# Two 64-wide halves of TensorE at a time in the stick-breaking and retention stages of a two-block model

## The reference, cut to what matters

```python
def retention(q, k, v):                      # 4 heads of 128
    s = einsum('bhid,bhjd->bhij', qi, ki) * decay[None]
    intra = einsum('bhij,bhjd->bhid', s, vi)
    ...
def stick_breaking(q, k, v):                 # 8 heads of 64
    z = einsum('bhid,bhsd->bhis', qi, kh) * scale
    past = kpos[None, :] < qpos[:, None]
    log_keep = where(past, log_sigmoid(-z), 0.0)
    between = cumsum(log_keep, axis=3, reverse=True) - log_keep
    a = where(past, exp(log_sigmoid(z) + between), 0.0)
    return einsum('bhis,bhsd->bhid', a, vh)
def even_mixer(x, w_in, w_out):
    ret = silu(rg) * normalised(retention(rotary(rq), rotary(rk), rv))
    return concatenate([ret, stick_breaking(sq, sk, sv)], -1) @ w_out
```

## Time and profile before

| | us |
|---|---|
| median of 3 runs | 3577.01 (3575.97 to 3581.78) |
| the profiled execution, its own time | 3577.77 |
| its span from first to last record | 3575.7 |
| PE busy / DVE / ACT / GpSimd | 3069.0 / 2069.7 / 847.5 / 695.4 |
| retention matmuls, 2274.7 to 2306.2 | 31.5 |
| normalisation of retention, 2306.2 to 2318.7 | 12.5 |
| stick-breaking, 2318.7 to 2414.5 | 95.8 |

### The profile page before, as it was taken

One profiled execution on the slowest core, in us unless ns is written; L12 is line 12 of the kernel. 1 busy time (PEld: TensorE's weight loads), 2 busy tenths in 40 slices (PEclk: granted clock), 3 DMA queues, 4 the chain that ended last, 5 costly groups with the idle time before them and its releaser, 6 DMA issues. The chain is left out here.

```text
span 3575.7 us, 35397 instructions
## 1 busy us (share of the span) xinstructions
PE 3069.0 (86%) x12578; PEld 2058.9 (58%) x12578; DVE 2069.7 (58%) x3639; ACT 847.5 (24%) x2182; POOL 695.4 (19%) x670
## 2 busy tenths in 40 slices
PE   6999888987777777777777789989999999899998
PEld 4887667773223222222222257667888777678886
DVE  2323775567776764684444455246875374768743
ACT  2112433123222222222222221241211012422101
POOL 0001443004444444444333311000000000200000
PEclk9999999999999999999999999989999999999999
DMA  7888896669999999999999942101332232023322
GB/s 246 283 268 272 244 295 217 198 234 422 421 421 421 419 414 421 416 409 420 417 421 420 419 169 90 43 1 48 109 96 90 93 100 65 1 83 94 99 88 71
DMA packets 154292, 845.78 MB, mean 237 GB/s; under 512 B 15328, under 2 KB 15584, under 8 KB 87584
## 3 DMA queue, kind: packets, MB, share of 16 engines
q0 software_dynamic: 79040, 561.28, 38.4%
q1 hardware_dynamic: 75104, 282.57, 25.2%
HBM read 841.70 MB, written 136.31 MB: 274 GB/s over the span
## 5 line engine op out<-in xcount | busy, mean ns | idle before, releaser
L798 PE MATMUL PS<-AR,HC 128*128 128x512 f32 x1536 | 721.1, 614 | 258.6 <-ACT HC L1272 257.2
L199 PE MATMUL PS<-AR_r,RHI 128*128 128x512 f32 x1888 | 752.3, 398 | 40.1 <-DVE AR_r L1444 13.6
L201 PE MATMUL PS<-AR_r,RING_r 128*128 128x512 f32 x1888 | 738.2, 391 | 0.0
L798 PEld LDWEIGHTS PS<-AR,HC 128*128 128x128 f32 x1536 | 281.1, 192 | 697.8 <-ACT HC L1272 404.1
L1627 DVE SCALAR_TENSOR_TENSOR AR<-AR 128x1024 f32<-128x1024 f32 x384 | 470.2, 1225 | 363.3 <-DMA AR<-peer_uv,XC 359.9
L200 PE MATMUL PS<-AR_r,RHI 128*128 128x512 f32 x1504 | 586.0, 390 | 0.0
L476 POOL DMA_INDIRECT AR<-peer_uv,XC x384 | 398.6, 1038 | 739.3 <-PE PS L798 547.8
L1426 DVE CAST RHI<-RING 128x1024 fp32r<-128x1024 f32 x256 | 178.7, 698 | 479.6 <-DMA RING<-in_wstream 476.9
L199 PEld LDWEIGHTS PS<-AR_r,RHI 128*128 128x128 f32 x1888 | 356.6, 189 | 124.8 <-issue 39.5
L201 PEld LDWEIGHTS PS<-AR_r,RING_r 128*128 128x128 f32 x1888 | 356.4, 189 | 75.1
L1428 DVE TENSOR_TENSOR RING_r<-RING,RHI 128x1024 fp32r<-128x1024 f32 x256 | 315.8, 1234 | 8.8
(11 more groups left out here) (336 smaller groups left out, 3492.4 us busy)
## 6 DMA issues: line engine op xcount, KB each, us to landing
RING<-in_wstream SPq DMA_DIRECT2D x304, 512.0 KB, 3.7
peer_uv<-in_peer_u SPq DMA_DIRECT2D x56, 1024.0 KB, 12.9
peer_uv<-in_peer_v SPq DMA_DIRECT2D x56, 1024.0 KB, 13.8
peer_uv<-in_peer_v POOLq DMA_DIRECT2D x8, 1024.0 KB, 13.3
peer_uv<-in_peer_u POOLq DMA_DIRECT2D x8, 1024.0 KB, 12.5
AR<-peer_uv,XC POOLq DMA_INDIRECT x384, 13.6
XL<-in_xl SPq DMA_DIRECT2D x1, 2048.0 KB, 9.4
RHI_f<-peer_uv,XC POOLq DMA_INDIRECT x128
```

The source lines that it names most:

```text
L199: pe.matmul(out, sh, mh, start=start, stop=False)
L201: return pe.matmul(out, sl, mh, start=False, stop=stop)
L798: mm = pe.matmul(bank(2 * (tt % 2) + x), DIAG[:, n % NDIAG, :], ROWS_UV[n % NROW][:, D + 512 * x:D + 512 * x + 512], start=(j == 0), stop= ...
```

## The change

Four things change.

1. Retention works on two heads at a time: `rt_scores(t)` makes the four matmuls of heads 2 pair and 2 pair + 1 alternately on the two row halves, into banks (0, 1) or (2, 7); `rt_values(t)` follows one step later with both heads. `SDEC` has four buffers in place of three.
2. GpSimd copies `SBQ` and `SBK` with four DMAs, right behind barrier 10, into `XC` and `HC` with the two halves of the partitions exchanged (512 KB each). The first `sb_scores` waits for all four. The four diagonal blocks of a head are computed from the exchanged copy, on the other 64 rows than the six later blocks, and the two kinds alternate in the order.
3. `sb_values(p)` computes two heads at a time, alternating the two halves of the output partitions, once for two heads. It stands behind `sb_weights(h)` of h = 2, 4, 6 and at the end, and `SBA` has three buffers. `sb_exp(h)` then waits for a values step only from h = 3 on.
4. DVE copies 128 partitions once for two heads (`sb_out(p)`), 4 copies in place of 8.

```diff
--- before.py
+++ after.py
@@ -315,7 +315,10 @@
         RO = EW[:, 0:2048].rearrange("p (a b) -> p a b", a=4)
         RSQ = HLF[:, 0:2048].rearrange("p (a b) -> p a b", a=4)
         RST = HLF[:, 2048:4096].rearrange("p (a b) -> p a b", a=4)
-        SBL, SBP, SBA = [HLF[:, 0:SBW], EW[:, 0:SBW]], [HLF[:, SBW:2 * SBW], EW[:, SBW:2 * SBW]], HLF[:, 2 * SBW:3 * SBW]
+        SBL, SBP = [HLF[:, 0:SBW], EW[:, 0:SBW]], [HLF[:, SBW:2 * SBW], EW[:, SBW:2 * SBW]]
+        SBA = [HLF[:, 2 * SBW:3 * SBW], ar(14336, SBW), ar(14336 + SBW, SBW)]
+        SBQ_TURNED, SBK_TURNED = (x.rearrange("p (a b) -> p a b", a=4) for x in (XCF, HCF))
+        RT_BANKS = [(0, 1), (2, 7)]
 
         eight = lambda a: ar(a, 4096).rearrange("p (a b) -> p a b", a=8)
         DQL, DKL = over("AR", F32R, [P, KT, S], 0), over("AR", F32R, [P, KT, S], 4096)
@@ -370,6 +373,7 @@
         gelu, weight_ready, gate_ready = sem("gelu"), sem("weight_ready"), sem("gate_ready")
         diag_ready, po_evac, po_t = sem("diag_ready"), sem("po_evacuated"), sem("po_transposed")
         strip_split = sem("strips_split")
+        sb_turned = sem("stick_breaking_halves_turned")
         rt = {k: sem(f"rt_{k}") for k in ("s", "d", "av", "o", "sum", "dev", "sq", "var", "root")}
         sb_const = sem("sb_constants_ready")
         st = {k: sem(f"sb_{k}") for k in ("z", "l", "read", "sp", "w", "a", "o", "ev")}
@@ -485,7 +489,11 @@
             pool.wait_ge(proj[1], 8)
             pool.wait_ge(s_even, 64)
             rotary(pool, steps, RK, RKR, HCF)
-            for n in range(10, 15):
+            barrier(pool, 10)
+            for src, turned in ((SBQ, SBQ_TURNED), (SBK, SBK_TURNED)):
+                for r, to in zip(HALVES, HALVES[::-1]):
+                    pool.dma_start(turned[to], src[r]).then_inc(sb_turned, 16)
+            for n in range(11, 15):
                 barrier(pool, n)
             pool.dma_start(STRIP, t["strips"]).then_inc(s_strip, 16)
             barrier(pool, 15)
@@ -821,31 +829,35 @@
             keep_clock(7, 8)
             barrier(pe, 10)
 
-            def rt_scores(i):
-                h, j = divmod(i, TT)
-                r = slice(64 * (h % 2), 64 * (h % 2) + 64)
-                if i >= 3:
-                    pe.wait_ge(rt["d"], i - 2)
+            def rt_scores(t):
+                pair, j = divmod(t, TT)
+                if t >= 2:
+                    pe.wait_ge(rt["d"], 2 * t - 2)
                 for x in range(2):
-                    a = 2 * (h // 2) + x
-                    mm = pe.matmul(bank(i % 3, 0, S - P * j), RKR[r, a, P * j:P * j + P], RQR[r, a, P * j:S],
-                                   start=(x == 0), stop=(x == 1))
-                mm.then_inc(rt["s"], 1)
-
-            def rt_values(i):
-                h, j = divmod(i, TT)
-                pe.wait_ge(rt["d"], i + 1)
-                if j == 0 and h >= 2:
-                    pe.wait_ge(rt["o"], h - 1)
-                pe.matmul(bank(3 + h % 2, P * j, S - P * j), RV[:, j, P * h:P * h + P], SDEC[i % 3][:, 0:S - P * j],
-                          start=(j == 0), stop=(j == TT - 1), skip_group_check=True).then_inc(rt["av"], 1)
-
-            n_rt = RET_HEADS * TT
-            for i in range(n_rt + 2):
-                if i < n_rt:
-                    rt_scores(i)
-                if i >= 2:
-                    rt_values(i - 2)
+                    a = 2 * pair + x
+                    for y, r in enumerate(HALVES):
+                        mm = pe.matmul(bank(RT_BANKS[t % 2][y], 0, S - P * j), RKR[r, a, P * j:P * j + P],
+                                       RQR[r, a, P * j:S], start=(x == 0), stop=(x == 1))
+                        if x == 1:
+                            mm.then_inc(rt["s"], 1)
+
+            def rt_values(t):
+                pair, j = divmod(t, TT)
+                for y in range(2):
+                    h = 2 * pair + y
+                    pe.wait_ge(rt["d"], 2 * t + y + 1)
+                    if j == 0 and pair == 1:
+                        pe.wait_ge(rt["o"], y + 1)
+                    pe.matmul(bank(3 + y, P * j, S - P * j), RV[:, j, P * h:P * h + P],
+                              SDEC[(2 * t + y) % 4][:, 0:S - P * j], start=(j == 0), stop=(j == TT - 1),
+                              skip_group_check=True).then_inc(rt["av"], 1)
+
+            rt_steps = RET_HEADS // 2 * TT
+            for t in range(rt_steps + 1):
+                if t < rt_steps:
+                    rt_scores(t)
+                if t >= 1:
+                    rt_values(t - 1)
             pe.wait_ge(rt["o"], RET_HEADS)
             for h in range(RET_HEADS):
                 pe.matmul(bank(h), ONES[:], RO[:, h, :], start=True, stop=True).then_inc(rt["sum"], 1)
@@ -859,14 +871,25 @@
             def sb_scores(h):
                 if h >= 2:
                     pe.wait_ge(st["a"], h - 1)
-                r, a, b = slice(64 * (h % 2), 64 * (h % 2) + 64), h // 2, 3 * (h % 2)
-                for j in range(4):
-                    pe.matmul(bank(b, P * j, P), SBK[r, a, P * j:P * j + P], SBQ[r, a, P * j:P * j + P],
-                              start=(j == 0), stop=True, skip_group_check=True)
-                for j, bb, at in ((0, b + 1, 0), (1, b + 2, 0), (2, b + 2, 256)):
-                    mm = pe.matmul(bank(bb, at, S - P * (j + 1)), SBK[r, a, P * j:P * j + P],
-                                   SBQ[r, a, P * (j + 1):S], start=(at == 0), stop=True, skip_group_check=True)
-                mm.then_inc(st["z"], 1)
+                if h == 0:
+                    pe.wait_ge(sb_turned, 64)
+                a, b = h // 2, 3 * (h % 2)
+                own, other = HALVES[h % 2], HALVES[1 - h % 2]
+
+                def score(j, k, q, r, bb, at, cols, start):
+                    return pe.matmul(bank(bb, at, cols.stop - cols.start), k[r, a, P * j:P * j + P], q[r, a, cols],
+                                     start=start, stop=True, skip_group_check=True)
+
+                def diagonal(j):
+                    score(j, SBK_TURNED, SBQ_TURNED, other, b, P * j, slice(P * j, P * j + P), j == 0)
+
+                score(1, SBK, SBQ, own, b + 2, 0, slice(256, S), True)
+                diagonal(0)
+                score(0, SBK, SBQ, own, b + 1, 0, slice(128, S), True)
+                diagonal(1)
+                diagonal(2)
+                diagonal(3)
+                score(2, SBK, SBQ, own, b + 2, 256, slice(384, S), False).then_inc(st["z"], 1)
 
             def sb_weights(h):
 
@@ -893,16 +916,17 @@
                 add(2, 128, 128, none, 1152)
                 add(2, 256, 128, none, 384).then_inc(st["w"], 1)
 
-            def sb_values(h):
-                pe.wait_ge(st["a"], h + 1)
-                if h >= 2:
-                    pe.wait_ge(st["ev"], h - 1)
-                r = slice(64 * (h % 2), 64 * (h % 2) + 64)
+            def sb_values(p):
+                pe.wait_ge(st["a"], 2 * p + 2)
+                if p >= 2:
+                    pe.wait_ge(st["ev"], p - 1)
                 for n, (j, at, a, w) in enumerate(((0, 0, 0, 128), (0, 128, 512, 384), (1, 128, 128, 128),
                                                    (1, 256, 896, 256), (2, 256, 256, 128), (2, 384, 1152, 128),
                                                    (3, 384, 384, 128))):
-                    mm = pe.matmul(bank(6 + h % 2, at, w)[r, :], SV[:, j, 64 * h:64 * h + 64], SBA[:, a:a + w],
-                                   start=(n == 0), stop=(n == 6), skip_group_check=True)
+                    for y, r in enumerate(HALVES):
+                        h = 2 * p + y
+                        mm = pe.matmul(bank(6 + p % 2, at, w)[r, :], SV[:, j, 64 * h:64 * h + 64], SBA[h % 3][:, a:a + w],
+                                       start=(n == 0), stop=(n == 6), skip_group_check=True)
                 mm.then_inc(st["o"], 1)
 
             sb_scores(0)
@@ -911,10 +935,10 @@
                     sb_scores(h + 1)
                 if h == 0:
                     keep_clock(7, 18)
-                if h >= 1:
-                    sb_values(h - 1)
                 sb_weights(h)
-            sb_values(SB_HEADS - 1)
+                if h >= 2 and h % 2 == 0:
+                    sb_values(h // 2 - 1)
+            sb_values(SB_HEADS // 2 - 1)
             barrier(pe, 12)
             keep_clock(5, 28)
 
@@ -1295,7 +1319,7 @@
 
             act.preload_act_table_set(LN_EXP)
             for h in range(RET_HEADS):
-                act.wait_ge(rt["av"], TT * (h + 1))
+                act.wait_ge(rt["av"], 2 * TT * (h // 2) + 2 * TT - 1 + h % 2)
                 act.activation(RO[:, h, :], bank(3 + h % 2), ACT.Copy).then_inc(rt["o"], 1)
             for h in range(RET_HEADS):
                 act.wait_ge(rt["dev"], h + 1)
@@ -1310,10 +1334,10 @@
 
             def sb_exp(h):
                 act.wait_ge(st["w"], h + 1)
-                if h >= 1:
-                    act.wait_ge(st["o"], h)
-                act.activation(SBA[:, 0:512], bank(3 * (h % 2)), ACT.Exp)
```

(29 more changed lines are left out.)

## The result

The changed kernel takes 3548.54 us (median of 4 runs, 3546.49 to 3551.51), the kernel before beside it 3576.49 us (4 runs, 3573.02 to 3581.78). The ratio is 0.9921, with a 95% interval of 0.9904 to 0.9938: 28 us faster. The forecast was 3550 with a range of 3541 to 3561. The profiled execution of the changed kernel took 3548.58 us, its span 3546.7, so span is compared with span: 3575.7 before, 29.0 less.

The account below looks back on a forecast made before the run. PE was taken to bound retention and stick-breaking, the latter with its Exp waits. Retention -10.4 and stick-breaking -16.3 make -26.7 us on 3577.8, 3551.1; the runs' median is 0.8 lower, so 3550, range 3541 to 3561.

Parts of the forecast that it names:

- Two halves at once: Both stages: a pair of passes on two row or column halves costs what one costs, read from neighbourhood attention.
- Each half runs through its own list: PE order: a pass on one half may start before an earlier-listed pass on the other half; no size given.
- Retention, -10.4: Retention stage: matmuls take 20.4 us, 11.0 less, and a second copy to RO adds 0.6, together -10.4 us.
- Copy at 0: Exchanged copy on GpSimd: lands in 9 to 36 us, needed after 33 us; charged 0, upper end costs 3 us.
- Stick-breaking, -16.3: Stick-breaking stage: 71.5 us at full clock plus 8 us for the lower clock, 79.5 against 95.8.
- full-clock list: Stick-breaking at 2.4 GHz throughout: rounds of 16.0 us for two heads, the last copy ending at 71.5 us.
- the chain takes over: Stick-breaking: an even head's chain of 16.0 us for two heads becomes the bound, above PE's own list of 11.5.
- 0 if idle is short enough, 15.4 if all stays: Stick-breaking: bounds in us on what TensorE's lower clock still costs after the change; half, 8 us, was taken.
- strict program order: Rival for score groups: matmuls start in order where PE has no backlog, adding 2.9 us, 3553 us; 12%.
- One kind does not pair: Rival: scores or values do not run in pairs, giving 3564 us without scores, 3560 without values; 8%.
- 1.2 GHz all through: Rival: half-array pairs count as little work, so both stages run at the lower clock, 3590 us; 3%.
- late copy: Rival: the exchanged copies land late, each us beyond 33 costing one us; 2%.

Follow-up runs that it names:

- filler run: The changed kernel with more clock-keeping matmuls in stick-breaking, 30 in place of 18 ahead of the first weights and others around later weights: 3546.18 us, ratio 0.9903.
- values single: The changed kernel with values again made one head at a time, one step behind the weights, out of one buffer: 3548.53 us, ratio 0.9913.
- scores alone: The kernel before with only stick-breaking's scores put on both row halves, from the exchanged copy; values and retention as before: 3559.8 us (before 3577.9).

## Why the prediction was right, and which of its terms were off

- **Bound by PE in both stages, savings kept**: right. 29.4 us were saved in the two stages, 29.0 in the span.
- **Two halves at once**: right for both kinds. The neighbourhood-attention rows were the right evidence, with a limit they could not show: they alternate. "Each half runs through its own list" was too much to read from one pass of the earlier trace rows: it has an end three passes ahead, the same for row and for column halves. The sum did not rest on it, since the change alternates.
- **Retention, -10.4**: measured -11.05. Scores 10.5 as said; values 10.5 for 10.8; 20.1 us of matmuls for 20.4. The second copy to RO, charged with 0.6, is there (L1323 x2, 1.08 us, PE idle 0.95 us ahead of L863, before 0.69 ahead of L851), but cost 0.3: the stretch from the last matmul to stick-breaking is 12.8 us for 12.5.
- **Copy at 0**: right, by 20 us. It would be 12 uncovered, near the lower end of the bounds given (9).
- **Stick-breaking, -16.3**: measured -18.3. The round was right: 16.2 and 16.1 with the clock held, for 16.0. The full-clock list ended at 71.5. The filler run takes 73.3; of that 0.7 are the fillers ahead of weights(5), and 0.8 its slower start (weights(0) at 11.3 where the change has 10.5), which leaves 71.8. So the mis-sized term is the clock's: half of 15.4 us, rounded to 8, where the change paid 6, by the list and by the slowed instructions on the chain alike (4.7 and 1.4 above). No run without any time at 1.2 GHz shows it. That the cost lay between the bounds is the forecast's; that half of it was near had no row behind it and is partly luck.
- **Two misses in the list that nearly cancel**: the odd heads were given 0.9 us of slack, but their Exp stands 0.9 us behind ACT's Ln of the next head, which the list did not have. And the chain from a head's scores to its weights is 10.45 us for 10.6.
- **A step that was wrong without moving the sum**: "the chain takes over" was credited to the change as a whole. By the prediction's own prices paired scores with single values in the old place need 8.25 us a head, 16.5 for two, against the chain's 16.0. Pairing the values and moving them behind the weights was worth half a us a round at full clock, and with the start and end of the stage 2.7 us where the clock was held in both. In the change the clock took that back: 24 us at 1.2 GHz, 3 with values single. Alone, values bring 6.2 us; beside paired scores, with the clock as it comes, nothing that can be measured.
- **"0 if idle is short enough, 15.4 if all stays"**: the clock followed both. PE idles 14.8 us of the stage before and 15.3 with values single; at about the same idle time, paired scores take the time at 1.2 GHz from 31 to 3 us (to 14 in the kernel with scores alone, 15.6 idle). Paired scores with more idle time, 18.2 us in the change, are at 1.2 GHz for 24, and with 4.9 us idle (more fillers) for 3 again. No kernel shows what exactly is counted, and the executions scatter: stages of the same stick-breaking code were at 1.2 GHz for 14 and 3 us (scores alone, values single) and lasted 79.9 and 76.1.
- **Rivals**: strict program order is out for both kinds of halves, by three passes of reach; for long runs on one half it is nearly right. "One kind does not pair" is out. 1.2 GHz all through is out, with clock 1.00 in retention. A late copy is out.
